# Attention scores of two heads as one full-array product in a hybrid decoder trunk

## The reference

```python
q = rms_norm(qkv[:, :, 0, g], q_gain[g]) * (ATTN_HEAD_DIM ** -0.5)
k = rms_norm(qkv[:, :, 1, g], k_gain[g])
...
scores = jnp.einsum('bnqrhe,bnkrhe->bnrhqk', qb, kk)
...
scores = scores + bias.astype(jnp.float32)[None, None, None]
scores = jnp.where(blk_valid[None, :, None, None], scores, -jnp.inf)
m = jnp.max(scores, axis=-1, keepdims=True)
ex = jnp.exp(scores - m)
den = jnp.sum(ex, axis=-1, keepdims=True)
out = jnp.einsum('bnrhqk,bnkrhe->bnqrhe', ex / den, vv)
```

## Time and profile before

| | |
|---|---|
| median of 3 runs | 3387.87 us (3387.51 to 3388.83) |
| profiled execution, span of the trace | 3382.0 us |
| PE busy | 3192.3 us (94%), 17466 instructions |
| PEld busy | 2669.5 us (79%) |
| DVE busy | 1334.0 us (39%) |
| ACT busy | 1102.1 us (33%) |
| POOL busy | 825.2 us (24%) |
| TensorE clock granted, mean | 0.978 |

### The profile page before, as it was taken

How to read it: one execution, slowest core, us unless ns; L and a number is a source line. 1 busy time by engine, 2 the same in 40 slices (tenths; PEclk the granted TensorE clock), 3 DMA queues, 4 the chain that set the end, 5 groups by cost and what they waited for, 6 DMA issues and landing times. The chain is left out here.

```text
span 3382.0 us, 48256 instructions
## 1 busy us (share of the span) xinstructions
PE 3192.3 (94%) x17466; PEld 2669.5 (79%) x17466; DVE 1334.0 (39%) x3725; ACT 1102.1 (33%) x3002; POOL 825.2 (24%) x598
## 2 busy tenths in 40 slices
PE   4999999999999995999999999899877999999999
PEld 3888888888888883878888888678655788888887
DVE  6445454555555554341313133541064431313131
ACT  4555555555555553321111112210244211111020
POOL 3332333333233320212222122112111122222221
PEclk9999999999999995999999999999998999999999
DMA  2112121211112114111111111111201111111112
GB/s 98 36 40 59 41 58 40 61 49 50 52 45 53 47 32 150 50 44 47 48 50 44 50 50 45 38 44 50 81 26 57 44 50 44 50 50 44 50 45 80
DMA packets 89904, 177.01 MB, mean 52 GB/s; under 512 B 25515, under 2 KB 55870, under 8 KB 89662
## 3 DMA queue, kind: packets, MB, share of 16 engines
q1 hardware_dynamic: 87358, 169.63, 16.1%
q10 hardware_dynamic: 2304, 4.20, 0.3%
HBM read 160.67 MB, written 13.12 MB: 51 GB/s over the span
## 5 line engine op out<-in xcount | busy, mean ns | idle before, releaser
L69 PE MATMUL ps_qk<-w_hi,attn_hT_hi 128*128 128x256 f32 x1536 | 437.4, 285 | 23.3 <-DVE attn_hT_lo L213 9.7
L915 POOL TENSOR_TENSOR first_w_lo<-first_raw,first_w_hi 128x1024 fp32r<-128x1024 f32 x96 | 231.7, 2414 | 900.8 <-ACT first_w_hi L911 900.8
L70 PE MATMUL ps_qk<-w_lo,attn_hT_hi 128*128 128x256 f32 x1536 | 436.1, 284 | 0.0
L71 PE MATMUL ps_qk<-w_hi,attn_hT_lo 128*128 128x256 f32 x1536 | 436.1, 284 | 0.0
L857 POOL TENSOR_TENSOR w_lo<-raw,w_hi 128x384 fp32r<-128x384 f32 x192 | 194.6, 1015 | 701.9 <-ACT w_hi L602 701.9
L915 POOL TENSOR_TENSOR second_w_lo<-second_raw,second_w_hi 128x1024 fp32r<-128x1024 f32 x72 | 172.2, 2391 | 630.0 <-ACT second_w_hi L911 630.0
L69 PEld LDWEIGHTS ps_qk<-w_hi,attn_hT_hi 128*128 128x128 f32 x1536 | 294.1, 191 | 27.6 <-issue 13.3
L635 ACT ACTIVATE prob<-ps_s,neg_max 128x128 f32<-128x128 f32 (+1 forms) x384 | 156.6, 413 | 439.7 <-DVE neg_max L726 439.7
L70 PEld LDWEIGHTS ps_qk<-w_lo,attn_hT_hi 128*128 128x128 f32 x1536 | 294.7, 192 | 0.4
L71 PEld LDWEIGHTS ps_qk<-w_hi,attn_hT_lo 128*128 128x128 f32 x1536 | 294.9, 192 | 0.0
L69 PE MATMUL first_ps<-first_hid_hi,first_w_hi 128*128 128x512 f32 x640 | 255.4, 399 | 32.7 <-DVE first_hid_lo L1239 32.7
(11 more groups left out here) (276 smaller groups left out, 6853.9 us busy)
## 6 DMA issues: line engine op xcount, KB each, us to landing
raw<-in_wqkv SPq DMA_DIRECT2D x192, 192.0 KB, 2.3
first_raw<-in_w SPq DMA_DIRECT2D x64, 512.0 KB, 3.4
second_raw<-in_w SPq DMA_DIRECT2D x64, 512.0 KB, 3.4
w_bc<-share_dram SPq DMA_DIRECT2D x48, 256.0 KB, 4.2
first_raw<-in_vo_pieces SPq DMA_DIRECT2D x16, 512.0 KB, 3.5
bias<-bias_dram SPq DMA_DIRECT2D x16, 256.0 KB, 3.6
yT_dram<-o_g SPq DMA_DIRECT2D x8, 512.0 KB, 3.1
first_raw<-in_attn_wo SPq DMA_DIRECT2D x8, 512.0 KB, 3.5
```

Of the source, the lines that this page charges most:

```text
L69: pe.matmul(out, a_hi, b_hi, start=first, stop=False)
L70: pe.matmul(out, a_hi, b_lo, start=False, stop=False)
L71: return pe.matmul(out, a_lo, b_hi, start=False, stop=last)
L915: pool.tensor_tensor(self.lo[:, n % 2, :], self.raw[:, n % self.RAW, :], self.hi[:, n % 2, :].bitcast(F32), ALU.subtract).then_inc(self.lo ...
```

## The change

- `qk_hi` and `qk_lo` (q and k together, 128 rows of which each head owns 64) become `q_hi`, `q_lo` as before for q, and `k_hi`, `k_lo` with a copy for each head: in the copy of head h the other head's 64 rows are zero. POOL writes these zeros once, with four memsets ahead of its first weight tiles (`blank`), for which PE waits once at the first scores.
- The scores of a unit are one `split_matmul` (three products) on all 128 rows, with both heads' keys as moving operand: 512 columns in a wide unit, 256 in a narrow one, in place of two of them (six products) on 64 rows.
- `ps_s` now holds both heads in one bank, and alternates between two banks with the unit; the wait of the scores is for the exp of two units back.
- ACT and DVE write q in one instruction of 128 partitions and k in two of 64 partitions: three instructions in place of two, on both engines.
- `ring` goes; `bias[0]` takes its place in the input's ring, and its first load waits for the end of that. The scratch for dynamic DMAs is set to 1024.

```diff
-        qk_hi = sb("qk_hi", [P, 2, 2, SEQ], F32R)
-        qk_lo = sb("qk_lo", [P, 2, 2, SEQ], F32R)
+        q_hi = sb("q_hi", [P, 2, SEQ], F32R)
+        q_lo = sb("q_lo", [P, 2, SEQ], F32R)
+        k_hi = sb("k_hi", [P, 2, 2, SEQ], F32R)
+        k_lo = sb("k_lo", [P, 2, 2, SEQ], F32R)
...
-        ps_s = [ps(f"ps_s{h}", [P, HALF]) for h in range(2)]
+        ps_s = [ps(f"ps_s{i}", [P, 2, 2 * P]) for i in range(2)]
...
-                    if st == 1:
+                    if st <= 1:
                         norm.wait_all(sp)
...
-                    if has_unit(st, j, 1):
-                        pe.wait_ge(exp_done, U)
+                    if st == 1 and j == 0:
+                        pe.wait_ge(blank, 4)
+                    if has_unit(st, j, 2):
+                        pe.wait_ge(exp_done, U - 1)
...
-                    for h in range(2):
-                        rows = slice(HD * h, HD * h + HD)
-                        mm = split_matmul(pe, ps_s[h][:, c0:2 * P],
-                                          qk_hi[rows, sp_, 0, u * P:(u + 1) * P], qk_lo[rows, sp_, 0, u * P:(u + 1) * P],
-                                          qk_hi[rows, sp_, 1, k0:(u + 1) * P], qk_lo[rows, sp_, 1, k0:(u + 1) * P],
-                                          True, True)
-                    mm.then_inc(scored, 1)
+                    split_matmul(pe, ps_s[u % 2][:, :, c0:2 * P],
+                                 q_hi[:, sp_, u * P:(u + 1) * P], q_lo[:, sp_, u * P:(u + 1) * P],
+                                 k_hi[:, sp_, :, k0:(u + 1) * P], k_lo[:, sp_, :, k0:(u + 1) * P],
+                                 True, True).then_inc(scored, 1)
...
-                            for a in range(2):
-                                ins = act.activation(perm_dest(qk_hi[:, sec % 2, a, :], g, t * P, P),
-                                                     perm_view(ps_t[:, a * P:(a + 1) * P], g, P), ACT.Copy,
-                                                     scale=gains[:, a, g:g + 1])
+                            act.activation(perm_dest(q_hi[:, sec % 2, :], g, t * P, P), perm_view(ps_t[:, 0:P], g, P),
+                                           ACT.Copy, scale=gains[:, 0, g:g + 1])
+                            for h in range(2):
+                                rows = slice(HD * h, HD * h + HD)
+                                ins = act.activation(perm_dest(k_hi[rows, sec % 2, h, :], g, t * P, P),
+                                                     perm_view(ps_t[rows, P:2 * P], g, P), ACT.Copy,
+                                                     scale=gains[rows, 1, g:g + 1])
...
+                            dve.scalar_tensor_tensor(
+                                perm_dest(q_lo[:, sec % 2, :], g, t * P, P), perm_view(ps_t[:, 0:P], g, P),
+                                gains[:, 0, g:g + 1], perm_dest(q_hi[:, sec % 2, :].bitcast(F32), g, t * P, P),
+                                ALU.mult, ALU.subtract)
+                            for h in range(2):
+                                rows = slice(HD * h, HD * h + HD)
                                 ins = dve.scalar_tensor_tensor(
-                                    perm_dest(qk_lo[:, sec % 2, a, :], g, t * P, P),
-                                    perm_view(ps_t[:, a * P:(a + 1) * P], g, P), gains[:, a, g:g + 1],
-                                    perm_dest(qk_hi[:, sec % 2, a, :].bitcast(F32), g, t * P, P), ALU.mult, ALU.subtract)
+                                    perm_dest(k_lo[rows, sec % 2, h, :], g, t * P, P), perm_view(ps_t[rows, P:2 * P], g, P),
+                                    gains[rows, 1, g:g + 1], perm_dest(k_hi[rows, sec % 2, h, :].bitcast(F32), g, t * P, P),
+                                    ALU.mult, ALU.subtract)
...
+            for n, (part, h) in enumerate(((k_hi, 0), (k_lo, 0), (k_hi, 1), (k_lo, 1))):
+                if n:
+                    pool.wait_ge(blank, n)
+                pool.memset(part[HD * (1 - h):HD * (2 - h), :, h, :].bitcast(F32), 0.0).then_inc(blank, 1)
+            pool.wait_ge(blank, 4)
```

More of the change, by code:

```diff
@@ L368, in attention_phase @@
         o_raw = [buffers.o_g0, total[:].rearrange("p (o t) -> p o t", o=1), buffers.o_g2]
-        ring = sb("ring", [P, HALF])
         compact = sb("compact", [64, NG, 2, 2, 16])
@@ L404, in attention_phase @@
         y_step, y_out = sem("y_step"), sem("y_out")
-        set_done, half_set = sem("set_done"), sem("half_set")
+        set_done, half_set, blank = sem("set_done"), sem("half_set"), sem("blank")
         norm = NormInput(nc, ctx, "attn", sem, buffers.x_tiles, total, norm_gain, ones,
-                         [ring[:], qkn[:].rearrange("p a c -> p (a c)"), bias[1][:].rearrange("p h k -> p (h k)")], [ps_p, ps_o], hT_hi, hT_lo)
+                         [bias[0][:].rearrange("p h k -> p (h k)"), qkn[:].rearrange("p a c -> p (a c)"),
+                          bias[1][:].rearrange("p h k -> p (h k)")], [ps_p, ps_o], hT_hi, hT_lo)
         block = ctx.enter_context(nc.Block())
@@ L634, in step @@
                     for h in range(2):
-                        a = act.activation(prob[:, u % 2, h, c0:2 * P], ps_s[h][:, c0:2 * P], ACT.Exp,
+                        a = act.activation(prob[:, u % 2, h, c0:2 * P], ps_s[u % 2][:, h, c0:2 * P], ACT.Exp,
                                            bias=neg_max[:, sp_, h * TT + u:h * TT + u + 1],
@@ L721, in step @@
                         rev = bass.AP(bias[g][:].tensor, h * width + n - 1, [[2 * width, P], [-1, n]])
-                        s = ps_s[h][:, 2 * P - n:2 * P]
+                        s = ps_s[u % 2][:, h, 2 * P - n:2 * P]
                         dve.tensor_tensor_reduce(s, s, rev, 1.0, -3.0e38, ALU.add, ALU.max,
@@ L860, in _ @@
             pool.memset(minus_half[:], -0.5).then_inc(half_set, 1)
+            pool.wait_ge(half_set, 1)
+            for n, (part, h) in enumerate(((k_hi, 0), (k_lo, 0), (k_hi, 1), (k_lo, 1))):
[3 more added lines that the diff above has]
+            pool.wait_ge(blank, 4)
             for k in range(KT):
@@ L1896 @@
     }
-    nc = bacc.Bacc("TRN2", target_bir_lowering=False, num_devices=1)
+    nc = bacc.Bacc("TRN2", target_bir_lowering=False, num_devices=1, dynamic_dma_scratch_size=1024)
     args = {n: nc.dram_tensor(f"in_{n}", a.shape, mybir.dt.from_np(a.dtype), kind="ExternalInput").ap()
```

## The result

| | us |
|---|---|
| before, median of 4 runs | 3387.69 (3383.65 to 3388.83) |
| after, median of 4 runs | 3505.15 (3501.00 to 3508.28) |
| ratio | 1.0348, 95% interval 1.0335 to 1.0361 |
| forecast | 3418, range 3394 to 3440 |
| span of the profiled execution, before and after | 3382.0 and 3504.6 |

A forecast was written before the change was run, and what follows sets the result against it. PE was taken to bound attention, with the ACT and DVE loop's slack used up: 0.0 + 4 x 4.85 + 2 x 3.83 + 2.95 = +30.0 us on 3387.9 gives 3418, range 3394 to 3440.

The forecast's parts named there:

- What bounds it, and the mechanism: Attention: PE sets the pace, busy 148.8 of 152.5 us per head pair; longer ACT and DVE work uses up the loop's slack.
- the loop through ACT and DVE: Each step's path from PE's transposes through DVE's maximum to exp's end: late 5.76 us wide, 5.19 narrow, against PE's 6.50 and 5.86.
- 3.65 and 3.56: Us from the end of a late exp on ACT to DVE's next maximum, after a wide and a narrow unit.
- PE's part: PE's score products: 0.34 us saved per narrow unit, 0.08 per wide one; upper bound of the gain 42 us.
- The wide product of rows 1024 apart: Rival, PE's wide scores: reading two key rows 1024 apart is slower, +20 us at a third more; no chance of its own.
- ACT's and DVE's part: Third q and k instruction in all 192 steps: 0.255 us on ACT, 0.26 on DVE, one after the other, 0.51 per step.
- The working: Step-by-step sum over a head pair's 24 units with merges and PE's waits: 157.2 us after against 152.4, +4.85 per pair.
- The clock: Rival: stops of up to 1.9 us at j = 0 halve PE's clock, +20 us on top, 3438; chance 0.03.
- POOL's memsets: Four memsets of 2048 columns before the first weight tiles: some 7 us, covered by POOL's wait for the first `w_hi`.
- Half hidden: Rival: only one of the two added instructions reaches the loop, -4 to -5 us, 3383; chance 0.10.
- all of it: Rival: the loop takes up all the added work without PE seeing it, -26 us, 3362; chance 0.07.
- The range: 3394 to 3440 us for the whole kernel, from the forecast's bounds (slower as forecast: +14 to +49), far ends left out.

The follow-up runs named there:

- The run with all partitions: Changed kernel with both copies of k written on all 128 partitions, a gain of zero on the other head's rows, on ACT and DVE: 3420.52 us.
- PE alone: Changed kernel with k written once, on all partitions, into copy 0 only, the separation of the heads left out: 3366.79 us, ratio 0.9938.
- the experiment on the last tile: Changed kernel with the keys of each section's last tile written once, on all 128 partitions, into copy 0: 3469.31 us, ratio 1.0241.
- The run with only ACT's writes mended: Changed kernel with ACT alone writing both key copies on all 128 partitions, DVE still in halves of 64: 3455.80 us, ratio 1.0205.

## Why the prediction was right and wrong

- **What bounds it, and the mechanism: right.** PE paces, the loop through ACT and DVE has 0.7 us of slack, and the change uses it up. The run with all partitions had the prices of the forecast and gave 3420.5, forecast 3418. (Two subtractions of the prediction, 3.65 and 3.56, are off by 0.01 and 0.02, without effect.)
- **PE's part: right.** 1.03 measured for 1.04 in the wide step, 0.12 for each narrow product, 19 to 21 us for PE alone where 25 were expected. The wide product of rows 1024 apart reads at 0.23 like any other, so that rival falls.
- **ACT's and DVE's part: wrong, and this is the step that failed.** I priced the third instruction at 0.255 and 0.26, with upper bounds of 0.317 and 0.302. It cost 0.50 and 0.47. I took the spacing of pairs that all start at partition 0, and the mean length per instruction as an upper bound. But the third instruction doesn't only add its own time: it breaks the overlap of two. The rows for it were in the trace of before, in the `ps_o` copies of 64 partitions on ACT, the only ones that change the start partition. They lie beside the transposes of the earlier trace rows:

```profile
584.96 0.25 ACT L651 COPY o_g<-ps_o 64x128 f32<-64x128 f32 x1
585.22 0.26 ACT L652 COPY o_g<-ps_o 64x128 f32<-64x128 f32 x1
585.50 0.51 ACT L602 CAST w_hi<-raw 128x384 fp32r<-128x384 f32 x1
586.04 0.38 ACT L667 ACTIVATE sq<-ps_qk 128x256 f32<-128x256 f32 x1
```

  The first copy, from partition 0, starts 0.10 before the end of the read ahead of it (584.86 + 0.20). The second, from partition 64, and the cast behind it, from 0 again, start only when the one ahead has ended, where L688 in the earlier trace rows starts 0.13 before the end of L684. With 0.255 from q to the first write of k and the full 0.374 for each of the two behind it, ACT's 0.51 becomes 1.00, as measured. The sentence "half the partitions do not make it shorter as far as the rows go" was true and the wrong question.
- **The working with the measured prices** gives +112, and with a start of attention 3 us later, 115 of the 122.6 us of span. It leaves the clock out. The first pair comes out at 158.4 us (trace 160.8), the later ones at 168.3 (trace 166.9).
- **The clock: a rival that came partly true, at 0.03.** I priced it at +20 and argued against it with a rest of 3 us at the end of a loop round that didn't lower it. The trace of before has a second such rest, of 2.96 us until 858.46, and behind that one the clock fell; I had read only the first:

```profile
850.00:865.00 15.00, 12.04 (x77) 10.65 (x75) 4.40 (x20) 6.87 (x25) 3.79 (x4) 0.89 0.11 32
```

  In the changed kernel it fell 16 times between 100 and 1300 us: behind 7 section starts (stops of 1.68 to 2.02 us), behind 7 waits for exp (1.91 to 1.98) and behind both ends of a loop round (3.9). PE lost 29 us by it against full speed, where the kernel before lost 1.7 up to its last section. Of the 29, 12 are those at the section starts, and the experiment on the last tile shows that they cost time (15 us beyond the lengths). How much of the other 17 reaches the time is open: behind a late exp the loop may set the pace anyway, and the working without the clock already gives 115 of the 122.6. The share of the clock in my range was too small in any case: I had forecast stops of up to 1.9 us myself, and the longest in the trace of before, but for the ends of the loop rounds, were 1.5.
- **POOL's memsets: the length right, the cover not.** Each took 1.80 us, 7.2 together, forecast 7. POOL was free again at 29.00, yet `w_lo` starts at 30.27, not 29.43, 0.84 later, and POOL waits 1.27 us for ACT's `w_hi` there. What I left out is DVE: its small instruction on `gains` ran beside the third memset, took 1.50 us where it takes 0.17 in the kernel before, and ended 0.03 after the memset. ACT's first `w_hi` came 0.76 later for it (29.62 for 28.86).

```profile
25.34 1.80 POOL L874 MEMSET k_hi<- 64x2048 f32 x1
25.67 1.50 DVE L708 TENSOR_SCALAR gains<-gains 128x3 f32<-128x3 f32 x1 [3.94 <-DMA gains<-in_k_gain]
...
30.27 4.30 POOL L866 TENSOR_TENSOR w_lo<-raw,w_hi 128x384 fp32r<-128x384 f32 x4 [1.27 <-ACT w_hi L603]
```

- **Half hidden, or all of it: wrong.** The run with only ACT's writes mended lies in the range of the sum of both engines' parts; 49 us go with ACT's 0.25 and 35 with DVE's 0.21.
- **The range** took its ends from the two wrong bounds. A cost for which no pair of rows is alike has to be bounded by the case without overlap as well: 0.37 and 0.36 for each of two instructions give +112 by the same working, an upper end of 3500. Even that lies 5 us under the 3505 measured; the later start and the clock are not in it.

## What to carry to other kernels

Before pricing an added instruction by the spacing of its neighbours, compare the start partitions along the queue: where they change (here between 0 and 64), it costs its full length, and so does the one behind it if they change back. A gain on the engine that sets the pace pays out only in the steps in which it still sets the pace afterwards; look for those steps, make the change in them alone, and put its cost on an engine that is idle there, at a time when its neighbour on the loop is not. If a forecast itself gives PE longer stops than the trace has, the clock is part of the forecast.

## What the runs showed of the hardware

- Behind a neighbour that starts at the same partition, the writes of q, k and v overlap by 0.11 to 0.14 us on ACT and by 0.07 to 0.09 on DVE, whether on 64 or on 128 partitions (spacing 0.25 and 0.26 for lengths of 0.37 and 0.35). They don't where the start changes from 0 to 64 or back (spacing 0.37 and 0.35). Nor does ACT's first read of PSUM from partition 0 overlap a cast out of SBUF if the last read of PSUM started at 64 (0.02 us or more between them, 82 times); it did by 0.09 before ACT's first read from partition 64 (once, at 61.31 us, in the kernel before).
- The clock fell to half pace behind 7 of 22 stops of PE at a section's start in the changed kernel (1.83 us in the one shown) and not behind the other 15, of 1.1 to 1.9 us, and behind one of the two rests of 3 us in the kernel before (granted clock 0.89 from 850 to 865 us, 1.00 around the other). What tells these apart wasn't tested.
- `neg_max`, 128x2 on DVE, takes 0.17 us, and 0.28 to 0.43 in 94 of the 138 cases beside a POOL product out of SBUF. `gains`, 128x3, takes 1.50 in place of 0.17 beside a POOL memset of 1.80 and ends with it.
- POOL's memset of 64x2048 elements takes 1.80 us; its product with a mask 0.40 us for 128x128 and 0.61 for 128x256.
